# Two-block transformer forward on one core: expert outputs added to the residual in DRAM by accumulating indirect transfers, entry of block two and overflow blocks pipelined

## What is computed

```
# block one
x = x + mixed @ w_out;  x = x + memory_cross_attention(...)     # 4 heads of 256, 256 memory rows
h = rms_norm(x, moe_norm_g)
x = x + hierarchical_moe(h, ..., w1, w3, w2)     # 32 experts, ff 512, top 2 of 8 in the best of 4 groups
x = rms_norm(x, final_norm_g)
# block two
z = _rmsnorm(x, norm_mix_g_2) @ w_in_2 ;  x = x + (SSM and forgetting attention, gated) @ w_out_2
x = x + _hier_moe(_rmsnorm(x, norm_ffn_g_2), ...)     # 32 experts, ff 256, top 2 again
# an expert: y += gate * ((silu(h @ w1) * (h @ w3)) @ w2)
```

## Time and profile before

| | before |
|---|---|
| median of 3 runs | 2154.24 us (2154.17 to 2158.22) |
| the profiled execution, its own time | 2158.92 us |
| its span in the trace | 2157.1 us |
| PE busy | 80% |
| DVE / ACT / POOL busy | 25% / 15% / 11% |
| moved by DMA | 463.17 MB |

### The profile page before, as it was taken

How to read it: one execution, slowest core, us unless ns; L and a number is a source line. 1 busy time by engine, 2 the same in 40 slices (tenths; PEclk the granted TensorE clock), 3 DMA queues, 4 the chain that set the end, 5 groups by cost and what they waited for, 6 DMA issues and landing times. The chain is left out here.

```text
span 2157.1 us, 19069 instructions
## 1 busy us (share of the span) xinstructions
PE 1716.9 (80%) x7266; PEld 873.0 (40%) x7266; DVE 545.9 (25%) x1211; ACT 323.2 (15%) x732; POOL 240.5 (11%) x272
## 2 busy tenths in 40 slices
PE   4997898888679778868878639797997987987872
PEld 2444676433334323322223225344743435543431
DVE  3375666110223310000010034313400005211112
ACT  1100442111222100000000020213400003100110
POOL 0120001459010100000000010010000001000001
PEclk9999899999999799988989869898998997988986
DMA  9212002321443699999999684621003055999985
GB/s 314 79 58 98 21 1 107 122 94 39 151 155 125 223 425 427 426 426 425 426 426 427 242 263 123 171 59 59 1 0 117 0 199 190 371 419 422 421 341 196
DMA packets 104345, 463.17 MB, mean 215 GB/s; under 512 B 9704, under 2 KB 17544, under 8 KB 78016
## 3 DMA queue, kind: packets, MB, share of 16 engines
q1 hardware_dynamic: 58320, 295.03, 35.6%
q10 hardware_dynamic: 35248, 127.30, 14.8%
q0 software_dynamic: 10688, 39.62, 5.5%
HBM read 419.44 MB, written 42.48 MB: 214 GB/s over the span
## 5 line engine op out<-in xcount | busy, mean ns | idle before, releaser
L1559 PE MATMUL ps<-ring,work 128*64 128x256 f32 (+1 forms) x2112 | 367.5, 504 | 15.1 <-DMA ring<-in_w_expert_up 10.2
L1575 PE MATMUL ps<-ring,work 128*64 128x512 f32 x784 | 224.6, 717 | 140.5 <-DMA ring<-in_w 87.9
L247 PE MATMUL ps<-hT,ring 128*128 128x512 f32 x640 | 283.5, 601 | 15.3 <-DMA ring<-in_w_in 12.0
L1559 PEld LDWEIGHTS ps<-ring,work 128*64 128x64 f32 x2112 | 162.9, 145 | 225.3 <-issue 179.8
L247 PEld LDWEIGHTS ps<-hT,ring 128*128 128x128 f32 x640 | 123.1, 193 | 171.6 <-issue 154.9
L1670 DVE TENSOR_TENSOR work<-work,ps 128x256 f32<-128x256 f32 (+1 forms) x64 | 22.7, 355 | 646.1 <-ACT work L1630 635.0
L1575 PEld LDWEIGHTS ps<-ring,work 128*64 128x64 f32 x784 | 62.1, 160 | 250.2 <-issue 114.9
L247 PE MATMUL ps<-work,ring 128*128 128x128 f32 (+3 forms) x832 | 133.0, 307 | 14.4 <-DVE work L2081 13.3
L247 PE MATMUL ps<-ring,hT 128*128 128x512 f32 (+1 forms) x320 | 124.8, 551 | 2.2 <-DVEq L231 1.4
L247 PEld LDWEIGHTS ps<-work,ring 128*128 128x128 f32 x832 | 112.8, 193 | 27.5 <-issue 23.0
L1188 PE MATMUL ps<-ring,hT 128*128 128x512 f32 x256 | 114.2, 601 | 1.9 <-DVEq L231 0.9
(11 more groups left out here) (403 smaller groups left out, 1674.5 us busy)
## 6 DMA issues: line engine op xcount, KB each, us to landing
ring<-in_w SPq DMA_DIRECT2D x66, 2048.0 KB, 14.2
ring<-in_w ACTq DMA_DIRECT2D x30, 2048.0 KB, 24.6
ring<-in_w_expert_gate SPq DMA_DIRECT2D x34, 1024.0 KB, 10.2
ring<-in_w_expert_up SPq DMA_DIRECT2D x34, 1024.0 KB, 13.8
ring<-in_w_expert_down ACTq DMA_DIRECT2D x28, 1024.0 KB, 28.1
ring<-in_w_in SPq DMA_DIRECT2D x13, 2048.0 KB, 15.2
ymid<-work ACTq DMA_DIRECT2D x132, 128.0 KB, 13.8
ring<-in_w_out SPq DMA_DIRECT2D x4, 2048.0 KB, 8.2
```

The source lines that it names most:

```text
L247: last = nc.tensor.matmul(out_, l, r, start=i == 0, stop=i == len(pairs) - 1)
L1559: last = nc.tensor.matmul(ps[64 * hf:64 * hf + 64, bank, 0:ff].rearrange("p (w n) -> p w n", w=2), xT[:, k, :], up[:, :, k * ff + hf * hw: ...
L1575: last = nc.tensor.matmul(ps[64 * hf:64 * hf + 64, bank, :], hT_[:, i % nch, 64 * (i // nch):64 * (i // nch) + 64], down[:, i, hf * 512:hf ...
```

## The change

- **Combine.** `ymid` and the gather back are gone. Ahead of the experts ACT writes the residual `x` to DRAM (`acc(m)`: the array `hres` in block one, the output itself in block two; 4 transfers of 512 KB). A second small product on PE (`gates_pe`) makes a table `gslot` of the gate of each slot, and ACT scales by it while it copies the expert's result out of PSUM. POOL then adds the 64 rows to DRAM with one indirect transfer that accumulates (`compute_op=ALU.add`). A row is two halves of 512, so the 128 partitions of a `yb` buffer are 128 half rows. POOL waits for each of these transfers before it issues the next.
- **Slots that are not used** now carry an index out of bounds, in the gathers and in the adds, and are skipped.
- **Entry of block two.** When POOL is through, SP reads the residual back from `hres`, and the final norm and the norm of block two are computed together, tile by tile, with no barrier. The factor of the final norm is applied to `x` only where the next residual is added (`r8`).
- **Overflow blocks** use two sets of places, so that their weights can be loaded while the last experts run, and both up products come ahead of both down products. The first gather for them is issued in the main stage.
- **End.** The output is complete when the last add has landed; the final store is gone.
- **Earlier.** On POOL `norm_pool("nm")` moves behind the fourth unit of the first loop, and `resnorm_pool("n5")` behind the second unit of the second. In `xattn_pe` the product with V comes one tile later, ahead of the SSM transposes, which now come ahead of the transposes of the probabilities; the row maximum is taken with its sign turned, one DVE operation less per tile. The store of 4 MB of zeros into `ymid` (at 38.7 us) is gone.

```
             for u in range(8):
+                if u == 4:
+                    norm_pool("nm", T)
...
-            resnorm_pool("n5")
...
+                if u == 2:
+                    resnorm_pool("n5")
...
+                j = i - 2
+                if j >= 0 and j % T == T - 1:
+                    h = j // T
+                    pe.wait_ge(S("x5_pT"), since("x5_pT") + j + 1)
...
+                if i < NX:
+                    s5_turn_pe(pe, i)
...
-                    dve.tensor_scalar(nmax[:, i:i + 1], rden[:, i:i + 1], -1.0, None, ALU.mult).then_inc(S("x5_max"), 1)
+                    dve.tensor_reduce(nmax[:, i:i + 1], ps[:, i % 2, 0:MEM], AX, ALU.min).then_inc(S("x5_max"), 1)
...
+                for t in range(T):
+                    act.dma_start(acc(m)[t * P:t * P + P, :], x[:, t, :]).then_inc(S(f"xinit{m}"), 16)
...
-                    nc.scalar.copy(yb[:, j % 4, :], ps[:, 6 + j % 2, :]).then_inc(S(f"yready{m}"), 1)
+                        n("yadd", 16 * (j - 3))
+                    nc.scalar.activation(yb[:, j % 4, :], ps[:, 6 + j % 2, :], ACT.Identity,
+                                         scale=gslot[:, j:j + 1]).then_inc(S(f"yready{m}"), 1)
                     n("yready", j + 1)
-                    for hf in range(2):
-                        act.dma_start(ymid[j * SLOT:j * SLOT + SLOT, hf * 512:hf * 512 + 512],
-                                      yb[64 * hf:64 * hf + 64, j % 4, :]).then_inc(S(f"store{m}_{j % 4}"), 16)
...
+            for j in range(4):
+                gather(j)
+            pool.wait_ge(S(f"xinit{m}"), since(f"xinit{m}") + 16 * T)
+            for e in range(NE):
+                pool.wait_ge(S(f"yready{m}"), since(f"yready{m}") + e + 1)
+                pool.indirect_dma_start(out=by_half(acc(m)),
+                                        out_offset=bass.IndirectOffsetOnAxis(ap=rowdst[:, e:e + 1], axis=0),
+                                        in_=yb[:, e % 4, :], in_offset=None, bounds_check=2 * SEQ - 1, oob_is_err=False,
+                                        compute_op=ALU.add).then_inc(S(f"yadd{m}"), 16)
+                if e % 2 == 1 and e // 2 + 4 < NE // 2:
+                    gather(e // 2 + 4)
+                if e == NE - 4:
+                    pool.wait_ge(S(f"planned{m}"), since(f"planned{m}") + 1)
+                    pool.wait_ge(S(f"xturned{m}"), since(f"xturned{m}") + NE // 2 - 3)
+                    over_gather(pool, m, rowtok[:, NE // 2:NE // 2 + 1])
+                pool.wait_ge(S(f"yadd{m}"), since(f"yadd{m}") + 16 * (e + 1))
...
-        def combine_pool(pool, m):
-            for j in range(8):
...
-        def combine_dve(dve, m):
...
+            for t in range(T):
+                act.wait_ge(S(f"xback_{t}"), 16)
+                square(t, xn[:, t, :], 2 * t)
+                act.wait_ge(S("n7_added"), since("n7_added") + t + 1)
+                square(t, x[:, t, :], 2 * t + 1)
+                if t:
+                    scale(t - 1)
...
+            def gained(t):
+                dve.wait_ge(S(f"xback_{t}"), 16)
+                dve.tensor_tensor(x[:, t, :], xn[:, t, :], final_g, ALU.mult).then_inc(S("n7_added"), 1)
...
-            for t in range(T):
-                dve.scalar_tensor_tensor(x_tile(t), x_tile(t), st[:, 16 + t:17 + t], final_g, ALU.mult, ALU.mult)
-            end_stage("dve", dve)
-            norm_dve("n7", x_tile, D, T, xn_tile, hT_tile, gains("mix2_g"))
-            end_stage("dve", dve)
+            gained(0)
+            gained(1)
+            variances(0)
+            gained(2)
+            scale(0)
+            variances(1)
+            turned(0)
+            scale(1)
+            gained(3)
...
-            sp.wait_ge(S("stage_done"), 3 * STAGES_TO_PART2)
+            sp.wait_ge(S("pool_over"), 1)
+            for t in range(T):
+                sp.dma_start(xn[:, t, :], hres[t * P:t * P + P, :]).then_inc(S(f"xback_{t}"), 16)
```

More of the change, by code:

```diff
@@ L33 @@
 NPAIR = NE // 2 + NOV // 2
-YROWS = (NE + NOV) * SLOT
 FF1 = 512
@@ L1687, in moe_pool, with gather @@
             pool.wait_ge(S(f"hmid{m}"), since(f"hmid{m}") + 16 * T)
-            for j in range(NE // 2):
+            def gather(j):
                 if j >= 4:
@@ L1812, in over_pool @@
                     pool.wait_ge(S(f"over{m}_turned"), i + 1)
                     step(pool)
[L1814 to L1819 removed]
+                    over_gather(pool, m, tokcol[:, 0:1])
```

439 lines of the change are left out of this document (255 added, 184 removed).

## The result

The changed kernel takes 2131.77 us (median of 4 runs, 2125.56 to 2133.64) against 2154.2 us before (4 runs, 2149.22 to 2158.22): ratio 0.9878, 95% interval 0.9861 to 0.9895. It is faster, but by 22 us where 82 were forecast, and 2132 lies above the range. Its profiled execution took 2133.31 us with a span of 2131.4, 25.7 less than before.

What follows compares the result with a forecast made beforehand. Expert stages were taken as bound by DMA bytes, with idle seams and small PE waits elsewhere. 8 + 7 + 12 - 3 + 20 + 38 = 82 us off the profiled 2158.92, less 4.7 to the median, gave 2072 us; 80% range 2046 to 2112.

Steps and rivals of the forecast that it cites:

- Part 1: Norm factors made earlier on POOL: the 9.12 us wait shrinks to 0.9 at most, 8 us gained, bounds 7.5 and 9.1.
- part 2: Cross-attention: the product with V no longer waits 2.00 us per head; 7 us gained.
- my upper bound of 13.6: Cross-attention gain in us if the product with V takes 3.70 us, as at the last head, instead of 5.40.
- Part 5: Entry of block two: last down product to SSM product in about 34.5 us against 55.3; 20 us gained, bounds 14 and 24.
- Part 3: DMA bytes in the two expert stages: 5.8 us gained per stage, 12 in all, bounds 32 gained and 47 lost.
- I take 0.62: DMA engine time in us per expert for the adds, counted as a read and a write, equal to the dropped stores.
- Part 4: Serial adds on POOL in stage two: 8.0 us per add against 8.35 us of stream per expert; 3 us lost.
- I take the middle, 7.2: Landing of an add in us, between a gather's 9.7 under full load and 4.6 with the engines free.
- The second rival: Adds pace stage two a little, landing like a gather under load: 9.5 us each, 2106 us in all; chance 0.15.
- Part 6: Overflow blocks and end: span ends at 2117.3 instead of 2157.1; 38 us gained, bounds 30 and 42.
- The stretch between: SSM and attention of block two, then second output projection to stage two's first up product: forecast gain 0 in each.

Runs made afterwards that it cites:

- x_front: Kernel before with only the new place of the norm factors in POOL's order and the cross-attention change: 2131.5 us, ratio 0.9883 to the kernel before.
- x_plain: Changed kernel with every add in both stages and overflow a plain indirect store, same waits, sums left out: 2054.8 us, ratio 0.9531 to the kernel before.
- x_planes69: x_planes9 with stage one done the same way, summed at the entry of block two: 2090.8 us, ratio 0.9681 to the kernel before.
- x_chains: Changed kernel, stage two's odd experts adding to a second tensor left out of the output, two adds under way: 2096.7 us, ratio 0.9723 to the kernel before.
- x_plain9: Changed kernel with plain indirect stores in stage two and its overflow only, same waits, sum left out: 2089.5 us, ratio 0.9684 to the kernel before.
- x_noskip: Changed kernel with the gathers' empty slots reading the last token's row instead of being skipped: 2147.0 us, ratio 0.9947 to the kernel before.
- x_planes9: Changed kernel, stage two storing plainly to two rows per token, summed at the end, overflow gather earlier: 2089.8 us, ratio 0.9706 to the kernel before.
- x_over8: Changed kernel with the first overflow gather issued eight experts before the end instead of four: 2130.3 us, ratio 0.9878 to the kernel before.
- x_quarters: Changed kernel with each stage-two up or gate matrix loaded by four transfers with 2 KB rows, not one with 8 KB: 2115.4 us, ratio 0.9811 to the kernel before.
- x_gfirst: Changed kernel with gathers ahead of the add in POOL's order and the first overflow gather earlier: 2158.8 us, ratio 1.0001 to the kernel before.

## Why the prediction was wrong

**Part 1 (POOL's order, 8 us) and part 2 (cross-attention, 7): right in mechanism, small in size.** Together 20.5 us; x_front shows that they last to the end. By the first up product of the other kernels, 700.2 to 708.9 us, it can be 18 to 27. The wait of 9.12 us went. A head takes 16.3 us (607.43 - 591.12) for 20.2, which is 3.9 us three times or 11.7; the product with V takes 3.60 us for 5.40, the condition of my upper bound of 13.6, and I had taken 7.

**Part 5 (entry, 20): right**, 20.6, with nearly each piece at its forecast place.

**Part 3 (bytes, 12): a term of the wrong size, little in stage one and more in stage two.** Each stage was to gain 5.8 us. Stage one lost 1.0. The step "I take 0.62 ... so the adds cost what the stores gave" was nearly right. An accumulating transfer costs more than a plain one of the same size by 12.5 us in 32 (x_plain), 9.1 (x_planes69, which also drops the wait and the residual's write) or 11.1 (stage two, x_chains less x_plain9), 0.28 to 0.39 us each. On one pass at 0.31 that makes an add 0.6 to 0.7 us where a pair of stores had been 0.62: with 0.70 it is 2.6 us lost in a stage instead of nothing. Skipping gave 4.9 us and not 6.8 (x_noskip). With the 1 us for the residual, 1.3 are left of 5.8. The kernel of parts 1 and 2 alone has the stage at 502.0, so 0.1 gained or 1.0 lost is what one execution can tell. A plain store in the add's place gains 12.6 against x_front, where 0.31 x 32 + 4.9 - 1 gives 13.8. The Trainium skill's price (Collectives: The Full Stack, section Part 3), two source reads for one, agrees in direction with the measured 6.2% against 3.9% of the engines' time on queue 0, gathers included; no run here shows the reads of an add apart.

In stage two the same term is 8.6 us off. With two chains, so without the serial wait, the loop takes 262.3 us for the 259.5 of the kernel before: 2.8 lost and not 5.8 gained. The adds above plain stores, 11.1 us, are the part of it that is shown; the rest is not taken apart.

**Part 4 (chain of adds, 3 us lost): this is the step that failed most.** I set "I take the middle, 7.2, and 0.8 for waking and adding: 8.0 us" against 8.35 us of stream per expert. The 0.8 was right. The landing was not: its mean is 8.2 us and its median 9.7, so the chain goes at 9.1 us per add, and at (2079.0 - 1821.4)/27 = 9.5 while the main loop runs. The 8.35 was too long as well: I had counted all 3.67 MB of an expert at 424 GB/s, 8.65 us, but the kernel before went at 259.5/32 = 8.1, since its queues moved only 102.6 MB in that window, 3.2 MB per expert, and the rest ahead of the first product. The stream goes at 7.8 us with plain stores (x_planes9) and at 8.2 with adds (x_chains). So instead of 0.35 us of room per expert the chain is about 1 us too slow, and 23.8 us are lost by the wait, not 3. I had also argued that a pacing chain would empty the queues and let landings fall towards 4.6 us. They do so only in part: the share is 0.91, nine of 28 adds landed in 8.1 us or less, the others in 8.6 to 11.3, and only the four after 2087 us took 3.6 to 4.7. The second rival, "an add lands like a gather under load", priced at 9.5 us and 2106, named this and had the 9.5; it had a chance of 0.15, and its time is still 26 us short, because parts 3 and 6 missed too.

The rule of the Trainium skill that I set aside there (DMA: Bandwidth & Descriptors, section Anatomy of one DMA), 2.0 us and bytes over 436 GB/s, would give 2.3 us; the lowest add landed in 3.6, the median in 9.7 in stage two and 14.1 in stage one.

**Part 6 (overflow and end, 38): 19.7.** The work on TensorE was forecast well, as x_planes9 shows where nothing is in its way. Two things were wrong. I left out that the end hangs on the same chain: the loop ends with four adds open, so the last add of the main loop lands 21 us after the last down product, and the overflow adds come behind it. x_over8 shows that the late gather, and the lost clock behind it, were not what cost. And I had 3.7 us for the tests and the closing, where 11.4 passed from the last landing (2120.0) to the end of the span: 4.6 for the tests, and 6.6 for POOL's closing DRAIN, for which I had 0.5. That is 7.7 of the 18.3 us that part 6 missed. The DRAIN was there before as well, from 2137.2 on, but it ran beside the combine and the final store, which the change takes away. In the kernels that, like this one, end with overflow adds or stores on POOL it takes 6.6 to 6.8 us.

**The stretch between, 7.6 us.** Not forecast. 2.4 us are the residual written ahead of the gathers (x_planes9, without it, takes 91.6 us from the projection for 94.0). In the 463.6 us of SSM and attention the granted clock was 0.93 for 0.95 and TensorE was busy 403.9 us for 399.2 with the same instructions, so this part is clock. Why it was lower is open: the eleven kernels with the new program took 461.2 to 467.3 us at 0.93 to 0.94, the kernel before and x_front 459.7 and 460.1 at 0.95 and 0.94, so it can be more than the difference of one execution from the next.

The sum: 5.5 and 0.6 us more than forecast; 6.8, 29.4 (parts 3 and 4 in stage two, 8.6 and 20.8), 18.3 and 7.6 us less. That is 82 - 56 = 26, the 25.7 of the profiles.

## What to carry to other kernels

An accumulating indirect transfer is not a store that also adds: in this kernel each had to land before the next was issued, so its landing time under the full load of the other queues, times the number of transfers, is a term of its own. Compare that with the time of the stream per step before anything else, with the landing under load and not a mean with the free one, and take the stream's time per step from a trace and not from all its bytes at the full rate. If it is near, give each contribution a row of its own, store plainly and add where VectorE is free; here this turned a gain of 1.2% into one of 2.9%. And in a chain in which each link waits for a landing and which sets the pace, work belongs behind the transfer and not in front. Last, look at what closes the program: a wait that lay under a final store comes to light when that store goes.

## What the runs showed of the hardware

- An accumulating transfer of 128 rows of 2 KB, half of them skipped: 1.57 us of issue on POOL against 0.99 plain. Landing, counted from the start of the issue, median 9.7 against 7.4 us beside rows of 4 and 8 KB (mean 8.2 against 7.0), and 14.1 against 9.7 beside rows of 8 and 16 KB (changed kernel, x_planes69); 3.6 at the least.
- On queue 0 it took the engines 6.2% against 3.9% of 470 us for the same megabytes, gathers included.
- Beside rows of 2 KB in place of 8 the add lands in 8.1 us instead of 9.7, but the engines were full at 365 GB/s (x_quarters) where they had been at 408 (x_planes9).
- The same serial wait cost 23.8 us in a stage of 32 adds (286.1 against 262.3) and 1.5 us in one of 32 plain stores (251.2 against 249.7). The links were 9.1 and 7.9 us apart on average, the stream at 8.2 and 7.8 us, with four buffers between; 2.3 us more of landing per transfer lie across that edge.
- Skipped slots are cheap but not free: with the gathers' unused half skipped queue 0 moved 30.76 MB for 39.15, stage one was 4.9 us shorter, and the chain of adds in stage two 7.2.
- POOL's DRAIN at the end of the program took 6.57 us in the changed kernel and five others, 6.73 in x_over8, 6.77 in x_gfirst and 8.24 in x_plain, with nothing left to run beside it. Where loads and stores still ran it was hidden (x_planes9, 4.64 us).
